# The triangular solve of the delta rule, spread from two quarters of the TensorE array to four

## The reference, cut to what matters

```python
def chunk_gated_delta_rule(q, k, v, g, beta):
    ...
    a_low = jnp.where(strict, jnp.einsum("bnhid,bnhjd->bnhij", k_beta, k) * decay, 0.0)
    eye = jnp.eye(CHUNK, dtype=jnp.float32)
    rhs = jnp.concatenate([v_beta, k_beta * jnp.exp(g)[..., None]], axis=-1)
    sol = lax.linalg.triangular_solve(a_low + eye, rhs, left_side=True, lower=True,
                                      unit_diagonal=True)
    ...
```

## Time and profile before

| what | value |
|---|---|
| runs, us | 984.96, 985.44, 993.21 |
| median, us | 985.44 |
| the profiled execution's span, us | 989.7 |
| mean granted TensorE clock in it | 0.992 of 2.4 GHz |
| PE, PEld, DVE, ACT busy, share of the span | 96%, 91%, 71%, 55% |
| chain that ended last | PE 78%, DVE 13%, ACT 5% |

### The profile page before, as it was taken

How to read it: one execution, slowest core, us unless ns; L and a number is a source line. 1 busy time by engine, 2 the same in 40 slices (tenths; PEclk the granted TensorE clock), 3 DMA queues, 4 the chain that set the end, 5 groups by cost and what they waited for, 6 DMA issues and landing times.

```text
span 989.7 us, 20130 instructions
## 1 busy us (share of the span) xinstructions
PE 945.6 (96%) x8542; PEld 897.8 (91%) x8542; DVE 704.9 (71%) x1106; ACT 548.7 (55%) x835; POOL 28.7 (3%) x71
## 2 busy tenths in 40 slices
PE   4899999989999999999989999999999999999996
PEld 2589998979999999799888999998899999999995
DVE  3689837577777766797875554466679789988845
ACT  3777323555544534856745444466675577766434
POOL 1200000000000000310100000000000000000000
PEclk9999999999999999999999999999999999999998
DMA  8944837538888788357433446543467546666941
GB/s 324 324 136 160 291 135 244 182 109 299 286 281 274 277 292 291 110 166 255 150 128 109 151 129 148 182 152 128 132 233 255 190 137 202 195 193 198 321 141 42
DMA packets 57401, 196.79 MB, mean 199 GB/s; under 512 B 6096, under 2 KB 10592, under 8 KB 57056
## 3 DMA queue, kind: packets, MB, share of 16 engines
q1 hardware_dynamic: 51840, 187.72, 56.2%
q10 hardware_dynamic: 5216, 7.53, 2.6%
q0 software_dynamic: 256, 0.26, 0.1%
HBM read 194.43 MB, written 1.06 MB: 198 GB/s over the span
## 4 chain that ended last, share of the span: by engine, by line
PE 78%; DVE 13%; ACT 5%; DMA 2%; issue 2%; ACTq 0%; SPq 0%; DVEq 0%
PE panel_banks L412 66%; DVE w_lo L1634 3%; PE work_banks L907 2%; DMA raw<-in_panels 2%; ACT w_hi L1083 1%; DVE mix_work L1980 1%; DVE raw L1667 1%; PE work_banks L878 1%; DVE gla_work L1753 1%; PE work_banks L618 1%; PE work_banks L591 1%; PE work_banks L678 1%; PE panel_banks L487 1%; PE work_banks L990 1%; PE work_banks L935 1%
## 5 line engine op out<-in xcount | busy, mean ns | idle before, releaser
L412 PE MATMUL panel_banks<-act_hi,w_hi 128*128 128x256 f32 (+1 forms) x1600 | 459.1, 287 | 10.7 <-DVE w_lo L1634 4.2
L412 PE MATMUL panel_banks<-act_lo,w_hi 128*128 128x256 f32 (+1 forms) x1600 | 450.7, 282 | 0.0
L412 PE MATMUL panel_banks<-act_hi,w_lo 128*128 128x256 f32 (+1 forms) x1600 | 450.3, 281 | 0.0
L1634 DVE TENSOR_TENSOR w_lo<-raw,w_hi 128x1024 fp32r<-128x1024 f32 x260 | 315.2, 1221 | 128.8 <-ACT w_hi L1083 127.4
L1083 ACT ACTIVATE w_hi<-raw 128x1024 fp32r<-128x1024 f32 x260 | 272.6, 1055 | 144.8 <-PE panel_banks L412 103.0
L412 PEld LDWEIGHTS panel_banks<-act_hi,w_hi 128*128 128x128 f32 x1600 | 303.9, 190 | 24.0 <-issue 16.2
L412 PEld LDWEIGHTS panel_banks<-act_lo,w_hi 128*128 128x128 f32 x1600 | 302.5, 189 | 1.8 <-issue 0.5
L412 PEld LDWEIGHTS panel_banks<-act_hi,w_lo 128*128 128x128 f32 x1600 | 302.5, 189 | 1.5
L412 PE MATMUL panel_banks<-hidden_hi,w_hi 128*128 128x256 f32 x352 | 97.9, 278 | 1.5 <-DVE w_lo L1634 1.2
L412 PE MATMUL panel_banks<-hidden_lo,w_hi 128*128 128x256 f32 x352 | 97.3, 276 | 0.0
L412 PE MATMUL panel_banks<-hidden_hi,w_lo 128*128 128x256 f32 x352 | 97.3, 276 | 0.0
(11 more groups left out here) (287 smaller groups left out, 985.3 us busy)
## 6 DMA issues: line engine op xcount, KB each, us to landing
raw<-in_panels SPq DMA_DIRECT2D x356, 512.0 KB, 5.2
mix_work<-delta_rows ACTq DMA_DIRECT2D x2, 1024.0 KB, 14.1
x_t<-in_x ACTq DMA_DIRECT2D x1, 1024.0 KB, 8.6
gla_work<-in_ctx_x ACTq DMA_DIRECT2D x1, 1024.0 KB, 11.9
mix_work<-in_rel_bias ACTq DMA_DIRECT2D x1, 1024.0 KB, 10.2
out_x<-ffn_work SPq DMA_DIRECT2D x4, 256.0 KB, 2.4
mix_work<-in_rel_bias ACTq DMA_DIRECT2D x1, 768.0 KB, 14.7
c_wide<-in_c_rows ACTq DMA_DIRECT2D x1, 512.0 KB, 5.1
```

The costliest lines, as they stand in the source:

```text
L412: ins = pe.matmul(out_, a, b, start=start and p == 0, stop=stop and p == 2, skip_group_check=True)
L1634: dve.tensor_tensor(wlo[:, v_ % PARTS, :], raw[:, u % RAW, :], whi[:, v_ % PARTS, :].bitcast(F32), ALU.subtract)\
```

## The change

Heads 4 to 7 move to the two off-diagonal quarters: their products read partitions 0 to 63 and write 64 to 127, or the other way round, so each product swaps the halves of these heads' blocks. PE issues for head i and head 4 + i four products in a row, one for each quarter. A tile's product now lies in two PSUM banks, heads 0 to 3 in one and 4 to 7 in the other, in the first or second half of the bank by the parity of the step. Steps 15 to 17 use two quarters that read the same partitions.

For heads 4 to 7 a product of T with a power of N lands in the other half than T itself. T2, T4 and T8 change: DVE adds the identity to the power ("lifted", `s_i`), PE multiplies by that, and ACT copies the result over `tt64`. N8 is no longer copied by ACT; DVE lifts it from PSUM. The masks at the start become four operations of 64x256 for a tile instead of two of 64x512, the identity additions move behind each tile's mask of step 0 (three operations for a tile), and the final subtraction of W (step 14) becomes four operations of 64x256 for a tile instead of two of 64x512. In steps 15 and 16 ACT makes two copies of 64x256 for a tile instead of one of 64x512.

```diff
 SOLVE = ["A", "N2", "N2T", "T2", "N4", "N4T", "T4", "N8", "T8", "T", "U", "W", "T", "U", "W", "T", "U", "W"]
-ADDED = [p for p, name in enumerate(SOLVE) if name in ("T2", "T4", "T8", "W")]
+LIFTED = [p for p, name in enumerate(SOLVE) if name in ("N2", "N4", "N8")]
+ADDED = [p for p, name in enumerate(SOLVE) if name == "W"]
+COPIED = [p for p, name in enumerate(SOLVE) if name not in ("N8", "W")]
+def solved(p):
+    return 4 * p + 4 if p < 15 else 60 + 2 * (p - 14)
...
+LOW, HIGH = slice(0, 64), slice(64, P)
+def solve_tile(t, p, m, half):
+    return MB[half, 2 * t + m // 4, p % 2 * 256 + m % 4 * 64:p % 2 * 256 + m % 4 * 64 + 64]
 def solve_step(t, p):
...
-    n, nt, w, tt = s_n[t], s_nt[t], s_w[t], tt64[t]
+    n, nt, w, one, tt = s_n[t], s_nt[t], s_w[t], s_i[t], tt64[t]
     whole = tt_[:, 8 * t:8 * t + 8, :]
-    lhs, rhs = {"N2": (nt, n), "N2T": (n, nt), "T2": (w, tt), "N4": (n, w), "N4T": (w, n), "T4": (nt, tt),
-                "N8": (w, nt), "T8": (n, tt), "U": (n, tt), "W": (nt, w)}.get(name, (None, None))
+    lhs, rhs = {"N2": (nt, n), "N2T": (n, nt), "T2": (one, tt), "N4": (n, w), "N4T": (w, n), "T4": (one, tt),
+                "N8": (w, nt), "T8": (one, tt), "U": (n, tt), "W": (nt, w)}.get(name, (None, None))
     if p == 0:
         pe.wait_ge(S("products_read"), 5 + t)
     elif p - 1 in ADDED:
         pe.wait_ge(S(f"added{t}"), ADDED.index(p - 1) + 1)
-    else:
-        pe.wait_ge(S(f"copied{t}"), p - len([q for q in ADDED if q < p]))
+    elif p - 1 in COPIED:
+        pe.wait_ge(S(f"copied{t}"), COPIED.index(p - 1) + 1)
+    if name in ("T2", "T4", "T8"):
+        pe.wait_ge(S(f"lifted{t}"), ("T2", "T4", "T8").index(name) + 1)
...
-    for m in range(8):
-        for half in ((slice(0, 64), slice(64, P)) if p < 15 else ((slice(64, P),) if name == "U" else (slice(0, 64),))):
-            o = MB[half, 2 * t + p % 2, m * 64:m * 64 + 64]
-            if p < 15 and lhs is None:
-                v = s_u[t][half, m, half] if p == 0 else tt[half, m, :]
-                ins = pe.matmul(o, v, ident[half, half], start=True, stop=True)
-            elif p < 15:
-                ins = pe.matmul(o, lhs[half, m, :], rhs[half, m, :], start=True, stop=True)
-            elif name == "T":
-                ins = pe.matmul(o, whole[half, m, 0:64], ident[half, half], start=True, stop=True)
+    for i in range(4):
+        if p < 15:
+            for m, half, to in ((i, LOW, LOW), (i, HIGH, HIGH), (4 + i, LOW, HIGH), (4 + i, HIGH, LOW)):
+                o = solve_tile(t, p, m, to)
+                if lhs is None:
+                    v = s_u[t][half, m, half] if p == 0 else tt[half, m, :]
+                    ins = pe.matmul(o, v, ident[half, half], start=True, stop=True)
+                else:
+                    ins = pe.matmul(o, lhs[half, m, :], rhs[half, m, :], start=True, stop=True)
+                if i == 3:
+                    ins.then_inc(S(f"solve_product{t}"), 1)
+            continue
+        for m in (i, 4 + i):
+            to = (HIGH, LOW)[(m < 4) != (name == "U")]
+            o = solve_tile(t, p, m, to)
+            if name == "T":
+                ins = pe.matmul(o, whole[LOW, m, 0:64], ident[LOW, LOW], start=True, stop=True)
             elif name == "U":
-                ins = pe.matmul(o, s_u[t][0:64, m, 64:P], nt[0:64, m, :], start=True, stop=True)
+                ins = pe.matmul(o, s_u[t][LOW, m, 64:P], nt[LOW, m, :], start=True, stop=True)
             else:
-                ins = pe.matmul(o, w[64:P, m, :], whole[64:P, m, 64:P], start=True, stop=True)
-            if m == 7:
+                ins = pe.matmul(o, w[HIGH, m, :], whole[HIGH, m, 64:P], start=True, stop=True)
+            if i == 3:
...
 for p in range(len(SOLVE)):
     for t in range(2):
-        dst = {"A": s_a, "N2": s_w, "N2T": s_n, "N4": s_nt, "N4T": s_w, "N8": s_n, "T": s_nt, "U": s_w}\
-            .get(SOLVE[p])
-        if dst:
-            act.wait_ge(S(f"solve_product{t}"), 2 * p + 2 if p < 15 else p + 16)
-            r = slice(0, P) if p < 15 else slice(64 * (p - 15), 64 * (p - 15) + 64)
-            act.activation(flat(dst[t][r]), MB[r, 2 * t + p % 2, :], ACT.Copy).then_inc(S(f"copied{t}"), 1)
+        if p not in COPIED:
+            continue
+        dst = {"A": s_a, "N2": s_w, "N2T": s_n, "T2": tt64, "N4": s_nt, "N4T": s_w, "T4": tt64, "T8": tt64,
+               "T": s_nt, "U": s_w}[SOLVE[p]][t]
+        c = p % 2 * 256
+        act.wait_ge(S(f"solve_product{t}"), solved(p))
+        if p < 15:
+            act.activation(flat(dst).rearrange("p (a b) -> p a b", a=2), MB[:, 2 * t:2 * t + 2, c:c + 256],
+                           ACT.Copy).then_inc(S(f"copied{t}"), 1)
+        else:
+            r = slice(64 * (p - 15), 64 * (p - 15) + 64)
+            other = slice(64 - 64 * (p - 15), 128 - 64 * (p - 15))
+            act.activation(flat(dst[r, 0:4]), MB[r, 2 * t, c:c + 256], ACT.Copy)
+            act.activation(flat(dst[r, 4:8]), MB[other, 2 * t + 1, c:c + 256], ACT.Copy)\
+                .then_inc(S(f"copied{t}"), 1)
...
+LOW, HIGH = slice(0, 64), slice(64, P)
+first_heads, last_heads = slice(0, 4), slice(4, 8)
 for t in range(2):
-    for half in (slice(0, 64), slice(64, P)):
-        ins = dve.scalar_tensor_tensor(s_nt[t][half], s_u[t][half, :, half], -1.0, over_tiles(m16t[half], 8),
-                                       ALU.mult, ALU.mult)
+    for half, heads, to in ((LOW, first_heads, LOW), (HIGH, first_heads, HIGH),
+                            (LOW, last_heads, HIGH), (HIGH, last_heads, LOW)):
+        ins = dve.scalar_tensor_tensor(s_nt[t][to, heads], s_u[t][half, heads, half], -1.0,
+                                       over_tiles(m16t[half], 4), ALU.mult, ALU.mult)
 then(ins)
-for t in range(2):
-    ins = dve.tensor_tensor(tt64[t], s_nt[t], over_tiles(ident64, 8), ALU.add)
-then(ins)
+def over_heads(v):
+    return v.unsqueeze(1).unsqueeze(1).to_broadcast([P, 2, 4, 64])
+def by_bank(v):
+    return v.rearrange("p (a b) c -> p a b c", a=2)
 for p, name in enumerate(SOLVE):
     for t in range(2):
         tt8 = tt_[:, 8 * t:8 * t + 8, :]
+        c = p % 2 * 256
+        prod = MB[:, 2 * t:2 * t + 2, c:c + 256].rearrange("p a (b c) -> p a b c", c=64)
         if p == 0:
             dve.wait_ge(S(f"copied{t}"), 1)
             dve.scalar_tensor_tensor(s_n[t], s_a[t], -1.0, over_tiles(m16, 8), ALU.mult, ALU.mult)\
...
+            dve.tensor_tensor(tt64[t][:, 0:4], s_nt[t][:, 0:4], over_tiles(ident64, 4), ALU.add)
+            for half, to in ((LOW, HIGH), (HIGH, LOW)):
+                dve.tensor_tensor(tt64[t][to, 4:8], s_nt[t][half, 4:8], over_tiles(ident64[half], 4), ALU.add)
+        if p in LIFTED:
+            if p < 7:
+                dve.wait_ge(S(f"copied{t}"), COPIED.index(p) + 1)
+                ins = dve.tensor_tensor(s_i[t], (s_w, s_nt)[p // 4][t], over_tiles(ident64, 8), ALU.add)
+            else:
+                dve.wait_ge(S(f"solve_product{t}"), solved(p))
+                ins = dve.tensor_tensor(by_bank(s_i[t]), prod, over_heads(ident64), ALU.add)
+            ins.then_inc(S(f"lifted{t}"), 1)
         if p in ADDED:
-            dve.wait_ge(S(f"solve_product{t}"), 2 * p + 2 if p < 15 else p + 16)
-            op = ALU.subtract if name == "W" else ALU.add
-            prod = MB[:, 2 * t + p % 2, :].rearrange("p (a b) -> p a b", b=64)
+            dve.wait_ge(S(f"solve_product{t}"), solved(p))
             if p < 14:
-                ins = dve.tensor_tensor(tt64[t], tt64[t], prod, op)
+                ins = dve.tensor_tensor(by_bank(tt64[t]), by_bank(tt64[t]), prod, ALU.subtract)
             elif p == 14:
-                for half in (slice(0, 64), slice(64, P)):
-                    ins = dve.tensor_tensor(tt8[half, :, half], tt64[t][half], prod[half], op)
+                for half, to in ((LOW, HIGH), (HIGH, LOW)):
+                    dve.tensor_tensor(tt8[half, 0:4, half], tt64[t][half, 0:4], prod[half, 0], ALU.subtract)
+                    ins = dve.tensor_tensor(tt8[to, 4:8, to], tt64[t][half, 4:8], prod[half, 1], ALU.subtract)
             else:
-                ins = dve.tensor_scalar(tt8[0:64, :, 64:P], prod[0:64], -1.0, None, ALU.mult)
+                dve.tensor_scalar(tt8[LOW, 0:4, 64:P], prod[LOW, 0], -1.0, None, ALU.mult)
+                ins = dve.tensor_scalar(tt8[LOW, 4:8, 64:P], prod[HIGH, 1], -1.0, None, ALU.mult)
```

More of the change, by code:

```diff
@@ L267, in two_blocks @@
             tt64 = [take(8, 64, at_=t_at + 4096 + 512 * n) for n in range(2)]
+            s_i = [take(8, 64, at_=m_at + 11264 + 512 * n) for n in range(2)]
             a21 = take(8, P, at_=t_at + 3072)
```

## The result

The changed kernel took 986.39 us at the median of 20 runs (978.35 to 994.58). The kernel before, timed in turn with it, took 992.90 (20 runs, 984.96 to 997.14). The ratio, which is taken from the fast runs and so is not just the quotient of the two medians, is 0.9943, 95% interval 0.992 to 0.9965: 0.6% faster. The forecast was 978.2 in 974.4 to 985.0. So the sign and the difference came out near (6.5 us between the medians, 7.2 forecast), and the time itself lies outside the range.

The account below looks back on a forecast made before the run. PE, busy for 96% of the span, bounds the kernel: 16.7 us saved, 7.1 given back in three waits, 2.4 to the clock, so 7.2 off the 985.44 median gives 978.2 us, range 974.4 to 985.0.

Parts of the forecast that it names:

- the last of the sum: Whole run: 7.2 us gain subtracted from the earlier runs' median of 985.44, giving 978.2 us.
- The products: Solve products on PE: four quarters overlap fully, saving 0.93 us a round, 16.7 us over 18 rounds.
- The rivals on quarters: Solve products: starts 27 ns apart, 982 to 984 us (0.13, shared with slow small operations); quarters take turns, 988 to 989.5 (0.07).
- The start: Before round 1: PE waits for DVE's masks, done at 526.1 and 528.0; rounds 0 and 1 keep 0.2 of 1.86 us.
- Round 5: Before round 5: PE stands 2.7 us for ACT's N4 copies; of 3.0 us saved so far, 0.9 is left.
- the train: On ACT before round 5: T2 copies, weight split, table load, Silu, table load, N4 copies; split begins at 535.2, awaiting its transfer.
- Round 15: Before round 15: PE waits 1.5, then 1.2 us for DVE's final subtraction; 2.0 us given back.
- The clock: After three PE standstills: half clock costs 0.8 us each, 2.4 in all, bounds 0 and 4.2.
- 9.6 stood: Whole solve: 9.6 us gained after the three waits if the clock costs nothing, 975.8 us; chance 0.2.

Follow-up runs that it names:

- keep_busy: Changed kernel with 20 spare products on PE ahead of the waits of round 1 (8, then 4) and round 5 (8); median 979.1 us, ratio 0.99 to before.
- masks_first: Changed kernel with both tiles' step 0 masks ahead of all six identity additions on DVE; median 981.4 us, ratio 0.9893 to before.
- all_three: Changed kernel with Silu and its table loads behind step 0, masks ahead of identity additions, last accumulation behind step 14's subtractions; 978.9 us, ratio 0.9858 to before.

## Why the prediction was wrong

**The step that failed** is the last of the sum: "The median of the runs is 985.44, 4.3 us less than that span, and I subtract from it", with a range that has bounds for every cost of the change and none for the runs. Two of those three runs turned out to be the quickest two of the twenty taken in turn with the changed kernel. The same kernel's medians in five turns are 992.9, 989.7, 990.8, 990.8 and 989.0, 3.5 to 7.5 us above. 992.9 less 7.2 is 985.7, against 986.39 measured. The three runs shown, 984.96 to 993.21, gave the warning: they spread by 8 us. The rest of the sum was near, 7.2 us forecast and 6.5 between the medians. Across three profiles of each kernel (the ones with spare products among them), the spans less pace are 978.2 before and 972.2 after on average, the solve's stretches 69.1 and 63.0: both 6 us apart, so no effect of the change outside the solve is seen.

**The products** were right: 1.09 us for 64 records, a round 2.66 instead of 3.58 us, 0.92 saved where 0.93 stood. The rivals on quarters fell with the same row. 64 records in 1.09 us are 17 ns each. The floor of about 25 ns between two starts that the Trainium skill (TensorE: Matmul & The Clock Gate, "Wait — 56ns, not 53.3ns?") states is contradicted by that. In rounds 16 and 17 two quarters that read the same partitions take 1.08 us for 32 records, so sharing rows cost nothing here.

**The start** was right to 0.15 us: first mask done at 526.23 (526.1 forecast), second at 528.14 (528.0). The small operations start 0.43 us apart (0.42).

**Round 5** was right as a mechanism, in its order (copies, split, load, Silu, load, copy) and in its transfer, and with PE kept busy late by 0.8 us, counted from the start of the solve, of which the longer transfer is 0.7. With the clock it came 2.1 us late, as half clock behind round 1 puts off T2's copies, and the train waits for them (537.53) rather than for the transfer: a coupling that the forecast lacked.

**Round 15** waited 1.0 and 1.1 us rather than 1.5 and 1.2, ended by the subtractions as said. A stop of 0.3 us for nothing that the profile shows, just ahead, took part of the first wait.

**The clock** was sized at 2.4 us, three falls of 0.8. The first profile had two, of 6.83 and 3.41 us. Their groups took 1.28, 0.73, 0.58 and 1.03 us longer than the rows at full clock: 3.6 us. Others had up to 17.1 us of half clock. But the kernel before loses to it too, in two of three profiles (69.7 and 69.6 against 68.1). Taking the quietest of each, 68.1 before and `keep_busy` less its 1.5 us behind round 15, 59.2 after, the change is worth 8.8 us without the clock where 9.6 stood; with it, 6.1 of the 7.2 (means of three profiles). `keep_busy` also stopped for 1.4 us of issue, against 0.3 in the changed kernel; without these 1.1 us the 8.8 would be about 10. By this estimate the clock took 2.7 to 3.9 us net where 2.4 stood. The term was somewhat small, and wrong in taking the kernel before to be free of it. That PE's own instructions could come late was no term of the sum at all: 0.3 us in the changed kernel, up to 3.3 where the waits had gone.

## What to carry to other kernels

Before subtracting a gain from a time, ask where in its own spread that time lies: three runs that differ by 8 us carry an offset larger than most single changes, and two profiles compared stage by stage show a 6 us gain that medians blur. A shorter round on the engine that bounds the kernel uncovers, one behind the other, the engines beside it, the clock and the supply of its own instructions, so moving the uncovered work (Silu, masks, an accumulation) was worth as much again as the change. Products meant to overlap on different quarters must stand next to each other in the program.

## What the runs showed of the hardware

- At granted clock 1.0, passes of 128x128 by 256 columns run at 113.3 or 117.8 ns, either for hundreds of passes, and change at interruptions; a spare product of 64 columns led to the quick pace each time, in five profiles.
- Half clock came behind standstills of 2.4 and 1.2 us (3.4 or 6.8 us long), of 2.2 us (3.4 us) and of 0.4 to 1.5 and 1.1 around round 15 (none, 3.4, 6.8 or 10.2 us in different profiles). It didn't always: none behind 2.8 us in `masks_first`, nor behind 2.4 and 1.5 in `all_three`. With spare products in the first two places there was none in the profile, and the mean clock of 8 runs was 0.991 rather than 0.987.
- PE stopped for 0.2 to 2.0 us at fixed record numbers of its program, whatever stood there, and went on 1.2 to 1.6 us after the end of one certain 16 KB transfer of its instruction queue; in the three profiles of the slower rounds of before it never did.
